# ScalarE's queue asks for adaLN's row tiles in place of SyncE's

## The reference

```python
for l in range(2):
    shift, scale, gate = split(c @ w_ada_mix[l] + b_ada_mix[l], 3)    # adaLN
    y = hybrid_mixer(x * (1 + scale) + shift)       # convolution group, attention group, w_out
    x = layer_norm(alpha * x + (1 + gate) * y) * ln1_g[l] + ln1_b[l]
    shift, scale, gate = split(c @ w_ada_ffn[l] + b_ada_ffn[l], 3)    # adaLN
    y = conv_gated_mlp(x * (1 + scale) + shift)     # w_up, conv of 3 on the gate half, SiLU, w_down
    x = layer_norm(alpha * x + (1 + gate) * y) * ln2_g[l] + ln2_b[l]
```

## Time and profile before

| | |
|---|---|
| median of 3 runs | 2138.21 us (2137.62 to 2140.28) |
| the profiled execution | 2137.87 us, its span 2135.9 us |
| PE busy | 2091.6 us, 98% of the span |
| POOL / DVE / ACT busy | 1403.7 / 1170.8 / 1034.0 us |
| row tiles asked for by SyncE | 80 of 512 KB |
| POOL's w_lo (L1742) | 1440 instructions, 1043.9 us |
| ScalarE's scalings (L1191) | 136 instructions of 715 ns |
| POOL's sums (L1814) | 102 instructions of 1301 ns |

### The profile page before, as it was taken

One profiled execution on the slowest core, in us unless ns is written; L12 is line 12 of the kernel. 1 busy time (PEld: TensorE's weight loads), 2 busy tenths in 40 slices (PEclk: granted clock), 3 DMA queues, 4 the chain that ended last, 5 costly groups with the idle time before them and its releaser, 6 DMA issues.

```text
span 2135.9 us, 27268 instructions
## 1 busy us (share of the span) xinstructions
PE 2091.6 (98%) x9585; PEld 1711.5 (80%) x9585; DVE 1170.8 (55%) x1898; ACT 1034.0 (48%) x1872; POOL 1403.7 (66%) x1769
## 2 busy tenths in 40 slices
PE   7999999999999999999999999999999999999996
PEld 7877778787888788888788888888778888888885
DVE  5798878675415554777532545587651454333224
ACT  3675356555515674364633656235552464333233
POOL 4977767755677887875557885564546776545553
PEclk9999999999999999999999999999999999999998
DMA  8645544533433354553233333332323232434332
GB/s 294 156 121 156 158 125 143 155 108 99 126 111 118 100 165 137 141 159 97 75 94 109 109 109 89 99 105 70 96 75 106 86 102 82 126 99 129 89 92 76
DMA packets 421221, 250.06 MB, mean 117 GB/s; under 512 B 48117, under 2 KB 393053, under 8 KB 421085
## 3 DMA queue, kind: packets, MB, share of 16 engines
q1 hardware_dynamic: 420218, 248.03, 39.3%
q10 hardware_dynamic: 867, 0.29, 0.1%
HBM read 242.71 MB, written 4.26 MB: 116 GB/s over the span
## 4 chain that ended last, share of the span: by engine, by line
PE 81%; POOL 6%; DVE 5%; ACT 3%; issue 2%; SPq 1%; DMA 1%; DVEq 0%; ACTq 0%; POOLq 0%
PE fg L807 26%; PE fg L809 26%; PE fg L808 25%; POOL w_lo L1742 3%; DVE bank_c L1413 2%; POOL ada_acc L1814 1%; PE bank_s L885 1%; ACT ada L1191 1%; SPq L651 1%; DMA first_ada<-in_w_ada_mix_dram 1%; PE bank_t L907 1%; PE bank_l L819 1%; PE bank_l L824 0%; PE bank_l L829 0%; PE bank_t L894 0%
## 5 line engine op out<-in xcount | busy, mean ns | idle before, releaser
L1742 POOL TENSOR_TENSOR w_lo<-raw,w_hi 128x256 fp32r<-128x256 f32 (+1 forms) x1440 | 1043.9, 756 | 665.9 <-ACT w_hi L1041 664.6
L807 PE MATMUL fg<-u_hi,w_hi 128*128 128x512 f32 x2112 | 841.7, 399 | 4.6 <-POOL w_lo L1742 1.6
L809 PE MATMUL fg<-u_hi,w_lo 128*128 128x512 f32 x2112 | 824.0, 390 | 0.0
L808 PE MATMUL fg<-u_lo,w_hi 128*128 128x512 f32 x2112 | 823.1, 390 | 0.0
L1041 ACT ACTIVATE w_hi<-raw 128x1024 fp32r<-128x1024 f32 (+2 forms) x392 | 379.5, 968 | 419.4 <-PE fg L809 321.8
L807 PEld LDWEIGHTS fg<-u_hi,w_hi 128*128 128x128 f32 x2112 | 397.1, 188 | 103.9 <-issue 18.4
L808 PEld LDWEIGHTS fg<-u_lo,w_hi 128*128 128x128 f32 x2112 | 397.4, 188 | 84.6 <-issue 5.0
L809 PEld LDWEIGHTS fg<-u_hi,w_lo 128*128 128x128 f32 x2112 | 396.9, 188 | 85.0
L1664 DVE SCALAR_TENSOR_TENSOR x<-fg,mod,x 128x512 f32<-128x512 f32 x160 | 120.0, 750 | 344.4 <-PE fg L809 344.2
L1413 DVE SCALAR_TENSOR_TENSOR bank_c<-glu,par,bank_c 128x512 f32<-128x512 f32 x448 | 305.8, 748 | 0.1
L807 PE MATMUL fg<-h_hi,w_hi 128*128 128x512 f32 x704 | 278.5, 396 | 0.0
(11 more groups left out here) (251 smaller groups left out, 1786.3 us busy)
## 6 DMA issues: line engine op xcount, KB each, us to landing
raw<-in_w_up_dram SPq DMA_DIRECT2D x176, 512.0 KB, 3.8
ada<-in_w_ada_ffn_dram SPq DMA_DIRECT2D x48, 512.0 KB, 4.5
raw<-in_w_down_dram SPq DMA_DIRECT2D x64, 384.0 KB, 3.5
raw<-in_w_in_dram SPq DMA_DIRECT2D x40, 512.0 KB, 3.9
raw<-in_w_down_dram SPq DMA_DIRECT2D x64, 320.0 KB, 3.1
ada<-in_w_ada_mix_dram SPq DMA_DIRECT2D x32, 512.0 KB, 4.5
raw<-in_w_in_dram SPq DMA_DIRECT2D x32, 256.0 KB, 3.8
raw<-in_w_out_dram SPq DMA_DIRECT2D x32, 256.0 KB, 3.0
```

Of the source, the lines that this page charges most:

```text
L807: pe.matmul(out[:], hi[:, k, :], rhi, start=k == order[0], stop=False)
L808: pe.matmul(out[:], hi[:, k, :], rlo, start=False, stop=False)
L809: ins = pe.matmul(out[:], lo[:, k, :], rhi, start=False, stop=k == order[-1])
L1742: ins = pool.tensor_tensor(w_lo[n % NRAW][:, ks, :], raw[n % NRAW][:, ks, :], w_hi[n % NHI][:, ks, :].bitcast(F32), ALU.subtract)
```

## The change

`load_ada` becomes a function of the queue that asks. SyncE keeps the requests up to m = 28, the first quarter of chunk 11. From there on ScalarE asks for m + 1 in the slot of m, right before it scales m, with the same wait for the sum of m - 1. 51 requests move (m = 29 to 79); their order, buffers and sizes stay.

```diff
+ADA_ON_SP = QUARTERS * (11 - CHUNKS_BEFORE)
...
+        def load_ada(queue, m):
+
+            c, part = CHUNKS_BEFORE + m // QUARTERS, m % QUARTERS
+            l, ffn, j = c // NCHUNK // 2, c // NCHUNK % 2, c % NCHUNK
+            if m >= 2:
+                queue.wait_ge(ada_add[added(m - 2)[0]], added(m - 2)[1])
+            src = a["w_ada_ffn" if ffn else "w_ada_mix"][l, part * 2 * P:(part + 1) * 2 * P, j * T:(j + 1) * T]
+            queue.dma_start(ada[m % 2][:], src.rearrange("(k p) n -> p k n", p=P)).then_inc(in_ada[m % 2], 16)
...
@@ SyncE's program @@
-            def load_ada(m):
...
-            load_ada(0)
+            load_ada(sp, 0)
...
                     if step[0] == "ad":
                         m = (step[1] - CHUNKS_BEFORE) * QUARTERS + step[2] + 1
-                        if m < QUARTERS * (4 * NCHUNK - CHUNKS_BEFORE):
-                            load_ada(m)
+                        if m <= ADA_ON_SP:
+                            load_ada(sp, m)
...
@@ ScalarE's program @@
-                    elif what == "ad" and step[1] not in DVE_CHUNKS:
-                        ada_scale(*step[1:])
+                    elif what == "ad":
+                        m = (step[1] - CHUNKS_BEFORE) * QUARTERS + step[2] + 1
+                        if ADA_ON_SP < m < QUARTERS * (4 * NCHUNK - CHUNKS_BEFORE):
+                            load_ada(act, m)
+                        if step[1] not in DVE_CHUNKS:
+                            ada_scale(*step[1:])
```

## The result

| | before | after |
|---|---|---|
| median | 2137.77 us (20 runs, 2135.33 to 2140.44) | 2140.65 us (20 runs, 2138.83 to 2144.56) |
| ratio of after to before, 95% interval | | 1.0014 [1.0008, 1.0020] |
| profiled execution, span | 2137.87, 2135.9 us | 2143.51, 2141.6 us |

The kernel became slower by 2.9 us (1.7 to 4.3), 0.14%. That is inside the prediction's range and under its border of 0.2%; the 1.7 us of its sum stand at the lower end of the interval. The profiled execution of after is one of its longer ones, so its 5.6 us over the profile of before are not the size of the effect.

What follows compares the result with a forecast made beforehand. TensorE, busy 98% of the 2135.9 us span, was taken as the bound. Terms 1.4 + 0.1 + 0.15 = 1.65 us, as 1.7, moved the median from 2138.21 to 2139.9 us; range 2137.4 to 2143.8.

Steps and rivals of the forecast that it cites:

- Slot 45's wait: 1.4: ScalarE waits for POOL before slot 45's scaling, 1.43 us late; reaches TensorE at chunk 12's sum: 1.4 us, bounds 0 to 1.5.
- The request: 0: ScalarE's 51 requests hide under the activation ahead of them: 0 each, bounds 0 and 0.37 + 0.04 us.
- Slots 49 to 51: 0.1: POOL's w_lo covers ScalarE's wait and scaling with 0.34 us to spare: 0.1 us, between 0 and 0.7.
- Slot 128: 0.15: Scaling 1.28 us late, mostly taken up by idle time, the rest delaying chunk 18's sum near 802 us: 0.15, 0 to 0.4.
- Taken away: SyncE loses 51 waits and requests; its standing still covers nothing: 0, with a gain of at most 1 us.
- the later tile: Tiles asked for when ScalarE arrives land later; a few scalings start up to 1 us late, outside critical stretches: 0.
- two queues: Row tiles run beside weights, not behind; a weight tile's landing could move 1 us either way: 0.
- The request in line: Rival: requests start only when ScalarE's engine is through, 0.41 us each, chiefly in attention beats: 2143.6 us, chance 0.17.
- Absorbed: Rival: slot 45's delay vanishes in VectorE's time between evacuations: 2138.2 us, chance 0.14.
- Weights sooner: Rival: w_hi starts up to 1 us earlier ahead of 381 us: 2137.4 us, chance 0.05.
- The lock: Rival: ScalarE's requests wait out SyncE's, 1.08 us in slot 45, eating slots 49 to 51's cover: 2141.8 us, chance 0.08.
- its 4.1 us of waits: TensorE's seven waits for norm sums, copied probabilities and adaLN's sums, 290 to 1210 us; little more could be won.

Runs made afterwards that it cites:

- before with the later sum: The kernel before the change, with TensorE's sum of chunk 12 one slot later: 2138.14 us, ratio 1.0001.
- the second request's with its tile last: The changed kernel plus an extra 4 KB request ahead of each of ScalarE's 51, its spare tile allocated behind all others: 2144.73 us, ratio 1.0032.
- The doubled request: The changed kernel plus an extra 4 KB request ahead of each of ScalarE's 51, its spare tile allocated between others: 2151.73 us, ratio 1.0063.

## Why the prediction was right, and where it was short

*Slot 45's wait: 1.4* was the bulk of the sum and held. Predicted: the scaling 1.43 us late, 0.4 us behind POOL's sum. Measured: 1.45 and 0.45. Predicted at TensorE: 1.4 us at chunk 12's sum. Measured: 0.6 us in slab 48 and 0.83 at the sum, together 1.4, in the kernel with only chunks 11 and 12 moved. (Measured from TensorE's end of slab 41, the scaling is 1.41 to 1.43 us later than before in four of the kernels with this wait.) One of the two places was not named: the delay reaches TensorE first through the probabilities, which the prediction passed on its way without asking who waits for them. In after's own profile slab 48 has no stall, because ScalarE is 0.57 us ahead already in slot 44, where no request delays it: against before, its w_hi is 1.04 us later (341.00 and 339.96) and TensorE's end of slab 41 is 1.61 later. TensorE had been held 0.5 us in slab 32. The profile of the kernel with slot 120's norm moved, which hasn't the change, shows the same wait in slab 32 and the same lead (w_hi 0.24 us later, TensorE 0.84), and that of before with the later sum has the lead without the wait. So it is a variation between executions, not shown to come from slab 32, and it is luck that after's own profile hides one of the two places. Who made TensorE wait from 254 to 266 us, after; before has no row there:

```profile
PE bank_l L821 <- POOL ssum L1876: 0.3, 1, 0.3
```

That the wait is the cause of what the slabs lose is shown four ways: chunks 11 and 12 back, or the request behind the scaling, takes the loss away; those chunks alone keep it; and slot 45's one request carries nearly all of it in the profile.

*A term that is missing is the clock.* The sum took a stall as worth its length. A longer stall is sometimes followed by 3.4 us at 1.2 GHz, 1.6 us more. The twelve profiles with the stall of slot 120 (about 2.5 us) show a fall behind it in four; of the five stalls of 1.4 to 2.2 us at slab 48 or chunk 12's sum two have one (after, and the second request's with its tile last), three haven't; and none followed the stall of 1.7 us in slab 274, in any profile. So a stall alone doesn't decide it. That the change's stall made falls more frequent is not shown: the mean clocks are 0.9940 against 0.9946, but two kernels without a longer stall at chunk 12's sum had 0.9938 and 0.9939, and falls in the first 55 us enter them. So the cost that is traced is 1.2 to 1.4 us, near the forecast's 1.65; the rest of the 2.9 us of the medians may be falls or scatter, and the interval reaches down to 1.7.

*The request: 0.* Right, for the reason given, in a sharper form. All 51 take 0.37 to 0.44 us; 35 of them lie wholly beside one running activation, those of slots 56 to 63 among them, and slabs 55 to 120 take 336.9 us in both kernels. The doubled request shows the margin: less than one more.

*Slots 49 to 51: 0.1.* Right in size. ScalarE's timeline of after:

```profile
369.94 1.34 ACT L1193 ACTIVATE ada<-ada,ccol 128x512 f32<-128x512 f32 x2 [1.98 <-POOL ada_acc L1816]
374.25 0.44 ACTq L621 DMA_DIRECT2D ada<-in_w_ada_mix_dram  x1
374.74 1.34 ACT L1193 ACTIVATE ada<-ada,ccol 128x512 f32<-128x512 f32 x2 [2.71 <-POOL ada_acc L1820]
```

The second scaling follows POOL's sum (over at 374.22) by 0.52 us, the first by 0.45, and POOL's w_lo covers them.

*Slot 128: 0.15.* Its two scalings came where they were put: 786.41 and 790.45 us, less the 5.64 us by which TensorE is later here, are 780.77 and 784.81, forecast 780.79 and 784.83. But nothing arrived at TensorE: slabs 122 to 136 take 73.8 us in both. The bound of 0 held. The list of slots in which ScalarE would wait for POOL missed two, 142 and 157 (0.4 us each); they too cost nothing.

*Taken away, the later tile, two queues: 0.* Nothing was won anywhere. Tiles land sooner by half a microsecond on ScalarE's queue (3.9 in place of 4.4), and TensorE's time shows nothing of it. This agrees with the rule quoted from the Trainium skill (DMA: Bandwidth & Descriptors, "Issuing engines are not separate DMA queues"), that another engine saves only sequencer time.

*The rivals.* The request in line is excluded: it would have put 0.4 us between tanh and the scaling in slot 56, and made slabs 55 to 120 longer. Absorbed: 0.57 us of the delay vanished in after's profiled execution, and none in the other profiles with slot 45's wait. Weights sooner: no trace of it. The lock: in after the request of 374.25 took 0.44 us in place of 0.37, with one of SyncE's at 374.22 beside it, and none of the 51 took longer. The rule of the lock that stood beside the sum (the Trainium skill, Perfetto Trace Analysis, "DMA Instruction — HWDGE") may hold, but between the two queues of this kernel it cost less than 0.1 us a request. Of the long requests on ScalarE's queue, which only the kernels with a second one show, most have none of SyncE's beside them, as at 672.63 us (1.26 us); what makes them long is open.

*What there was to win.* The prediction held that more than its 4.1 us of waits couldn't be won. Two norms and a sum moved by a slot won 5.1. Its waits are idle times, shorter than the stalls (2.1 and 0.4 us for 2.52 and 0.83); the earlier trace rows leave out 1.1 us of waits for POOL's w_lo; and they end at 1210 us, ahead of slab 274's 1.4.

## What to carry to other kernels

Here a request for a transfer cost ScalarE nothing while an activation ran that was longer than it (0.60 against 0.37 us); the semaphore that the request waits for holds up everything behind it on the engine (1.45 us in slot 45). Put such a request behind the work that doesn't need it, not ahead. And when a change moves 3 us in 2100, look first at who makes TensorE wait: two norms and one sum asked for a slot later were worth more, 5.1 us, than all that the queues could give or take.

## What the runs showed of the hardware that was not expected

- After a stall of TensorE of 1.4 to 2.7 us the granted clock was 1.2 GHz for 3.4 us in six cases and 2.4 GHz in eleven (at slab 48, chunk 12's sum and slot 120), with stalls of 2.5 us in both. A fall costs 1.6 us, and two of them are as large as the effect under study.
- Near the kernel's start, where TensorE also waits, the time at 1.2 GHz ran from 3.3 to 13.2 us between profiles, and cost little: 32 matmuls in 10 us at a mean clock of 0.51, 34 at 0.83. A run's mean clock doesn't tell the one kind of fall from the other.
- In the attention beats of slots 56 to 63 ScalarE's requests started 0.01 to 0.12 us after the start of the activation ahead of them. A second one right behind stuck out by 0.43 us in a gate slot.
- Moving one small allocation in the on-chip memory changed the time by 7 us (2151.73 and 2144.73), mostly in stages that had no part in the edit. A spare tile in an experiment belongs at the end.
